# Moving the FFN's h and the second-stage weights by 64 bytes, and all that lies behind by 128

## The reference, cut to what matters

```
h = rms_norm(x, mix_norm);  z = h @ w_in          # 1024 x 6696: inputs of four mixers, and their gates
x = x + merged(four mixers of z, gates) @ w_out
h = rms_norm(x, ffn_norm)
x = x + (silu(h @ w_gate) * (h @ w_up)) @ w_down  # hidden width 2816
```

## Time and profile before

| | us |
|---|---|
| median of the runs | 778.85 |
| the profiled execution's own time | 779.07 |
| its span | 777.3 |
| TensorE (matmuls) busy | 772.2 |
| VectorE busy | 568.7 |
| ScalarE busy | 389.9 |
| GpSimd busy | 89.6 |

### The profile page before, as it was taken

The page is one execution under the profiler, slowest core; times in us unless marked ns, Lnnn a source line. Parts: engine busy times, 40 slices in busy tenths (PEclk is TensorE's granted clock), DMA queues, the critical chain, the costliest instruction groups (busy, mean ns, idle before and its releaser), DMA issues.

```text
span 777.3 us, 11535 instructions
## 1 busy us (share of the span) xinstructions
PE 772.2 (99%) x4600; PEld 681.6 (88%) x4600; DVE 568.7 (73%) x794; ACT 389.9 (50%) x587; POOL 89.6 (12%) x97
## 2 busy tenths in 40 slices
PE   8999999999999999999999999999999999999998
PEld 8988888888888888888888899999889999999886
DVE  5536987889888965334435799789989778787991
ACT  6645545355573564443333465555544555555430
POOL 7100040335003211211310000000000000000000
PEclk9999999999999999999999999999999999999999
DMA  8362213221133231514244054326073333338202
GB/s 276 105 186 82 80 55 109 79 85 55 58 105 109 63 100 55 217 55 119 98 136 146 18 178 146 101 97 214 3 253 106 102 108 109 109 110 288 91 28 82
DMA packets 66629, 87.72 MB, mean 113 GB/s; under 512 B 1988, under 2 KB 52496, under 8 KB 66576
## 3 DMA queue, kind: packets, MB, share of 16 engines
q1 hardware_dynamic: 65680, 85.86, 33.5%
q0 software_dynamic: 752, 0.99, 0.5%
q10 hardware_dynamic: 144, 0.13, 0.1%
HBM read 81.21 MB, written 4.19 MB: 110 GB/s over the span
## 4 chain that ended last, share of the span: by engine, by line
PE 99%; DVE 0%; issue 0%; POOL 0%; ACT 0%; DVEq 0%; POOLq 0%
PE bank L2009 18%; PE bank L2010 17%; PE bank L2011 17%; PE bank L2458 9%; PE bank L2460 9%; PE bank L2459 9%; PE bank L2519 5%; PE bank L2521 5%; PE bank L2523 5%; PE bank L2285 1%; PE bank L2117 1%; PE bank L2255 1%; PE bank L2244 1%; PE bank L2276 1%; PE bank L2189 1%; PE bank L2381 0%
## 5 line engine op out<-in xcount | busy, mean ns | idle before, releaser
L2009 PE MATMUL bank<-h_hi,w_hi 128*128 128x512 f32 (+1 forms) x416 | 155.9, 375 | 0.1
L2011 PE MATMUL bank<-h_hi,w_lo 128*128 128x512 f32 (+1 forms) x416 | 153.7, 369 | 0.0
L2010 PE MATMUL bank<-h_lo,w_hi 128*128 128x512 f32 (+1 forms) x416 | 153.5, 369 | 0.0
L1280 DVE TENSOR_TENSOR w_lo<-raw,w_hi 128x2048 fp32r<-128x2048 f32 x36 | 85.3, 2375 | 53.0 <-ACT w_hi L742 45.4
L2009 PEld LDWEIGHTS bank<-h_hi,w_hi 128*128 128x128 f32 x416 | 78.5, 189 | 13.2 <-issue 0.4
L2011 PEld LDWEIGHTS bank<-h_hi,w_lo 128*128 128x128 f32 x416 | 78.4, 188 | 13.3
L2458 PE MATMUL bank<-t_hi,w_hi 128*128 128x256 f32 x320 | 89.8, 281 | 0.0
L2010 PEld LDWEIGHTS bank<-h_lo,w_hi 128*128 128x128 f32 x416 | 78.5, 189 | 12.7
L2459 PE MATMUL bank<-t_lo,w_hi 128*128 128x256 f32 x320 | 89.4, 279 | 0.0
L2460 PE MATMUL bank<-t_hi,w_lo 128*128 128x256 f32 x320 | 89.4, 279 | 0.0
L742 ACT ACTIVATE w_hi<-raw 128x2048 fp32r<-128x2048 f32 x34 | 65.2, 1921 | 15.3 <-PE bank L2011 15.0
(11 more groups left out here) (294 smaller groups left out, 1730.7 us busy)
## 6 DMA issues: line engine op xcount, KB each, us to landing
raw<-in_w_in_dram SPq DMA_DIRECT2D x26, 1024.0 KB, 5.1
raw<-in_w_ffn_gate_dram SPq DMA_DIRECT2D x11, 1024.0 KB, 5.2
raw<-in_w_ffn_up_dram SPq DMA_DIRECT2D x11, 1024.0 KB, 5.2
raw<-in_w_ffn_down_dram SPq DMA_DIRECT2D x7, 1024.0 KB, 5.0
raw<-in_w_branch_dram SPq DMA_DIRECT2D x4, 1024.0 KB, 4.9
raw<-in_w_out_dram SPq DMA_DIRECT2D x4, 1024.0 KB, 5.0
b<-in_w_ffn_down_dram SPq DMA_DIRECT2D x4, 1024.0 KB, 6.7
x_sb<-in_x_dram SPq DMA_DIRECT2D x4, 512.0 KB, 5.7
```

Source lines behind the costliest of these rows:

```text
L1280: vec.tensor_tensor(w_lo[:, at], raw[:, c % 2, 0:n], w_hi[:, at].bitcast(F32), ALU.subtract)\
L2009: mm(dst, l_hi, r_hi, start=start, stop=False)
L2010: mm(dst, l_hi, r_lo, start=False, stop=False)
L2011: return mm(dst, l_lo, r_hi, start=False, stop=stop)
```

## The change

The FFN's high and low h get tiles of their own names, 64 bytes behind H0; the mixer's h stays where it was. The four weight blocks of the second down stage move by the same 64 bytes. The space grows by 128 bytes, and so `raw` and all that is placed behind it moves by 128. The rest of the diff only passes the new names to the code of the FFN.

```diff
         h_hi = place("h_hi", [P, KT, SEQ], F32R)
         h_lo = place("h_lo", [P, KT, SEQ], F32R)
 
-        b11, b21, b12, b22 = (place(f"b{n}", [P, CHUNK], at=H0 + i * 8 * KB) for i, n in enumerate((11, 21, 12, 22)))
+        f_hi = place("f_hi", [P, KT, SEQ], F32R, at=H0 + 64)
+        f_lo = place("f_lo", [P, KT, SEQ], F32R, at=H0 + 64 + 16 * KB)
+        top[0] += 128
+
+        b11, b21, b12, b22 = (place(f"b{n}", [P, CHUNK], at=H0 + 64 + i * 8 * KB) for i, n in enumerate((11, 21, 12, 22)))
         raw = place("raw", [P, 2, CHUNK])
@@ h2_high (ScalarE)
-                    nact.activation(h_hi[:, ks, t * P:(t + 1) * P],
+                    nact.activation(f_hi[:, ks, t * P:(t + 1) * P],
@@ h2_low (VectorE)
-                    vec.tensor_tensor(h_lo[:, ks, t * P:(t + 1) * P],
+                    vec.tensor_tensor(f_lo[:, ks, t * P:(t + 1) * P],
                                       bank[4 + 2 * (t % 2) + half][:, :].rearrange("p (k t) -> p k t", t=P),
-                                      h_hi[:, ks, t * P:(t + 1) * P].bitcast(F32), ALU.subtract)\
+                                      f_hi[:, ks, t * P:(t + 1) * P].bitcast(F32), ALU.subtract)\
@@ first gate chunk
-                        last = three(b[:, cols], w_hi[:, w], w_lo[:, w], h_hi[:, k, cols], h_lo[:, k, cols],
+                        last = three(b[:, cols], w_hi[:, w], w_lo[:, w], f_hi[:, k, cols], f_lo[:, k, cols],
@@ first up chunk (rows_chunk takes the two tiles as arguments)
-            rows_chunk(first + 1, CW, up_bank)
+            rows_chunk(first + 1, CW, up_bank, f_hi, f_lo)
@@ wino_chunk
-                            r_hi, r_lo = (h[:, of_h[0].start + k, of_h[1]] for h in (h_hi, h_lo))
+                            r_hi, r_lo = (h[:, of_h[0].start + k, of_h[1]] for h in (f_hi, f_lo))
```

More of the change, by code:

```diff
@@ L2016, in take_bank, with rows_chunk @@
                 return bank[f % 2]
-            def rows_chunk(c, cols, bank_of):
+            def rows_chunk(c, cols, bank_of, right_hi=h_hi, right_lo=h_lo):
                 for j in range(cols // P):
@@ L2022, in rows_chunk @@
                         w = slice(w_at(c) + k * cols + j * P, w_at(c) + k * cols + (j + 1) * P)
-                        last = three(b[:, :], w_hi[:, w], w_lo[:, w], h_hi[:, k, :], h_lo[:, k, :],
+                        last = three(b[:, :], w_hi[:, w], w_lo[:, w], right_hi[:, k, :], right_lo[:, k, :],
                                      k == 0, k == KT - 1)
```

## The result

| | before | after |
|---|---|---|
| median of 6 runs each, us | 778.93 | 782.03 |
| lowest to highest | 778.64 to 779.23 | 781.38 to 783.17 |
| the profiled execution's own time | 779.07 | 782.34 |
| its span | 777.3 | 780.6 |

The kernel became slower: after / before is 1.0043 [1.0033, 1.0053]. The forecast was 777.15 us, with a range up to 779.0.

A forecast was written before the change was run, and what follows sets the result against it. It took TensorE's matmul pace as the bound, busy 772.2 of 777.3 us with almost no waits. Terms -1.8, -0.17 and +0.3 summed to -1.7, from 778.85 to 777.15 us; range 776.7 to 779.0.

The forecast's parts named there:

- (4): Mixer matmuls with h: moving to 128 apart modulo 256 changes nothing, 0 us; priced from 6.6 us added to -6.6.
- rival A: Mixer: alikeness modulo 256 or 512 counts, so its matmuls slow by 6.6 us; about +4.9 overall, 783.8 us; chance 0.12.
- sign rule: Mixer: rival A decides the sign as soon as a fourth of its 1104 matmuls with 512 columns go over.
- (1): FFN's 20 chunks: h products reach the T pace, 1.8 us off, or 1.6 if the irregular h-T step stays.
- (2): First gate chunk: about 75 matmuls of 256 columns gain 2.2 ns each, 0.17 us off.
- (3): First up chunk: 48 matmuls of 512 columns go over to the slower kind, 0.3 us added.
- (5): Products with stationary a, mg and T: relations of places unchanged, 0 us.
- (6): VectorE and ScalarE: stay hidden behind TensorE; if cover failed in one stage, 0.8 or 1.2 us of gain lost.
- (7): DMA: same packets, raw moves by 128 and b by 64 bytes, transfers stay hidden, 0 us.
- rival C: Down stages: TensorE arrives earlier and waits for split weights or a load, losing 0.8 to 1.2 us; chance 0.04.
- B: Rival for all TensorE matmuls: place doesn't matter, time stays at 778.85 us; chance 0.06.

The follow-up runs named there:

- experiment 1: Bare list without the layer: 42 segments of 48 equal fp32r matmuls, stationary tile shifted; with 512 columns 226.7 ns at distance 256, 232.5 at 128.
- experiment 2: Changed kernel with 256 bytes put in ahead of raw in place of 128: 775.53 us, ratio to before 0.9959.
- experiment 4: Changed kernel with the FFN's h back at H0 and 64 bytes ahead of raw in place of 128: 781.80 us, ratio to before 1.0036.
- experiment 6: Changed kernel with 256 bytes ahead of raw in place of 128 and the mg tiles 192 bytes further on: 773.37 us, ratio to before 0.9936.
- experiment 9: experiment 6's kernel, waiting for T tiles one product later, last weights of the first down stage 64 bytes further on: 776.11 us, ratio to before 0.9966.

## Why the prediction was wrong

**The step that failed is (4), the mixer, put at 0.** It rested on the sentence that pairs 64 and 192 apart modulo 256 behave alike, and on the inference that the pattern is therefore 128 bytes long. Both halves fall. In the bare list they are not alike: 233.5 against 229.2 ns with 512 columns (experiment 1). mg lies at 64 as reckoned here, and its 233.3 fits the first. iq against ik is the pair at 192, and its 233 doesn't fit the second; these few matmuls, with a stationary operand of 96 rows, step unevenly in the trace of before (232 to 237 ns), and why they don't run at 229 stays open. And likeness of 64 and 192 says nothing of 128: a pattern of 256 bytes in which both lie off its best place has it too. The two rows that I took as evidence against rival A fit it equally well. The 0 was the middle of a range of 13 us over 1104 matmuls on the path; with no row that shows a pair 128 apart, it should not have held 0.74 of the chance.

**Rival A was the right mechanism**, at 0.12: 783.8 us forecast by it, 782.03 measured. Its price was mis-sized. It had 7.3 - 0.7 = 6.6 us for the mixer, at 6.6 ns for each matmul of 512 columns; the bare pace gives 5.8 ns and 6.0 us, and the two profiled executions with this mixer 5.04 and 5.88, or 5.70 and 5.71 without what their starts differ by. In regular stretches of the kernel the step is 6.9 ns (226.7 to 233.6), so some of the 1104 matmuls pay less; which ones was not followed. Its sign rule was sound: it needed a fourth of these matmuls.

**(1)** The 20 chunks: -1.83 us measured, -1.8 forecast, with chunks of 9.894 us against 9.895. The irregular step between h and T went, as the forecast's larger value assumes. The number was right, but partly by luck: term 1 assumed that one distance has one pace, and the same distances gave 113.3 ns in experiments 2 and 4.

**(2)** and **(3)** were right: -0.15 against -0.17, and +0.29 against +0.3. **(5)** a, mg and T kept their paces. **(6)** and **(7)**: no new wait of TensorE; rival C did not occur, and neither did B. In experiments 2, 6 and 9, where TensorE comes into the first chunk faster still, the cover of (6) did fail once, for 0.4 us: VectorE's seeding, behind its weight sums, came too late for S1.

The prediction set aside the Trainium skill, "SBUF — State Buffer", section "Who interferes with whom", where TensorE's read ports for the moving operand and for the weight load are called independent. Experiment 1 speaks against taking this to mean that places don't count: 226.7 to 234.0 ns for one shape with no wait, by nothing but the place of the stationary operand. Why the distance of the two counts, no run here shows.

**What stays open:** what decides in the kernel whether the chunks are entered at 113.3 or at 117.8 ns, and why after itself varies by 1.8 us where before varies by 0.6. The first may be a cause of the second, and so may the opening transposes, which set the profiled executions apart by up to 0.9 us; only one execution of each kernel was profiled.

## What to carry to other kernels

Where TensorE is the bound and never waits, compare start-to-start times of equal shapes; unequal ones point to where the operands lie, and a change of one constant in the layout can be worth more than a change of the order of work. A shift for one stage moves every pair behind it: list each pair's distance modulo 256 before and after, and measure the ones that no row shows before relying on an interpolation. Here 512 moving columns want distance 0 and 256 columns rather 64, 128 or 192 (at 64 or 192 113.3 or 117.8 ns, at 128 118.5, at 0 120.0), so tiles shared by stages of both kinds should get a place of their own for each.

## What the runs showed of the hardware

- With 512 moving columns the fp32r pace depends on the distance of the operands modulo 256: 226.7 ns at 0 up to 234.0 at 96. At a distance of 16 bytes it was 226.9 too, at 32 already 232.9. With 128 columns it hardly counts: 110.6 to 111.7.
- With 256 columns, 0, 96 and 160 bytes are the slowest (119.8 to 120.2), and 64 and 192 each have two lasting paces, 113.3 and 117.8 ns. Which of them a segment gets depends on what ran before it, and a stall of 0.4 us ended the faster one in two kernels and not in a third. At 113.3 the 1680 matmuls of the 20 chunks would take 7.6 us less than at 117.8; in no profiled execution did it hold beyond the first eight.
- The granted clock was 1.00 in these stretches, its 2.4 GHz level. At that level the paces are whole cycles, worked out: 226.7 ns is 544, 120.0 is 288, 113.3 is 272, 233.3 is 560, so the steps are 16 cycles apart; 117.8 and 229.2 lie between such steps.
